# Three pieces of the expert behind a pair are worked between the pair's last two piece pairs

## The chip, the cores and the metric

The kernel runs on one core of one Trainium2 chip. Its time is device microseconds of one launch, and the numbers below are the median of three runs and one profiled execution.

## The reference

The program computes one block with four sequence mixers and a mixture of experts, and a second block behind it. The change touches the mixture alone. Of the reference that is:

```python
D_MODEL = 1024; SEQ = 512; N_EXPERTS = 32; TOP_K = 4; D_EXPERT = D_MODEL
SWIGLU_LIMIT = 7.0; SWIGLU_ALPHA = 1.702

def _moe_ffn(x2d, router_w, router_b, w_gu, b_gu, w_down, b_down):
    logits = (x2d @ router_w + router_b).astype(jnp.float32)
    top_val, top_idx = lax.top_k(logits, TOP_K)
    gate = jax.nn.softmax(top_val, axis=-1)
    ...
    def expert_block(args):
        xblk, e = args
        hg, hl = jnp.split(xblk @ w_gu[e] + b_gu[e], 2, axis=-1)
        hg = jnp.minimum(hg, SWIGLU_LIMIT)
        hl = jnp.clip(hl, -SWIGLU_LIMIT, SWIGLU_LIMIT)
        glu = hg * jax.nn.sigmoid(hg * SWIGLU_ALPHA)
        return ((hl + 1.0) * glu) @ w_down[e] + b_down[e]
    yb = lax.map(expert_block, (xb, block_expert)).reshape(n_rows, d)
    y = (yb * row_gate[:, None]).astype(x2d.dtype)
    return jnp.zeros((t + 1, d), x2d.dtype).at[row_tok].add(y)[:t]
```

Each token goes to 4 of 32 experts. An expert's weights are 1024x2048 and 1024x1024 floats, 12 MB, and all 32 experts' weights are read once: 384 MB.

## The kernel before

**Pieces.** An expert's weights come in 12 pieces of 1 MB (128 partitions x 2048 floats, CHUNKS = 12). Pieces 0 to 7 are the first product (banks `pu`, two pieces to a bank), pieces 8 to 11 the second (banks `pd`). Each expert gets a tile of 128 token rows; the few that need more have their other rows done elsewhere (`RestOfExperts`).

**Singles and pairs.** The 14 experts with the fewest tokens are worked two at a time: 64 rows for the left, 64 for the right, as fp32 products of half width straight from the loaded pieces. That is a *pair*, 24 pieces. The other 18 are *singles*. A single's piece is split first: ScalarE rounds it into `wh` (`high_part`), VectorE subtracts into `wl` (`low_part`), and TensorE adds up twelve products (`wh` and `wl` with `Xh`, `wh` with `Xl`). The order of units is ORDER = 4 x "sssp" + 3 x "ssp": 25 units, numbered by place from 0; the pairs stand at places 3, 7, 11, 15, 18, 21 and 24. A single that follows a pair is called `behind`; there are six. Places 4 to 15 are three turns of a loop.

**Buffers.** Eight slots hold loaded pieces (`raw` and a part of `y`, `slot_of`). A pair has eight more, `more_raw`, and these lie on the memory of `wh` and `wl`: slots 0 to 3 of `more_raw` are the four slots of `wh`, slots 4 to 7 those of `wl`. A pair's pieces 0 to 7 go to the eight slots, 8 to 15 to `more_raw`, 16 to 19 to four of the eight slots again, 20 to 23 to `more_raw` again (`pair_slot`). Piece pair 10 (pieces 20 and 21) lies on slot 2 of `wh` and `wl`, piece pair 11 (22 and 23) on slot 3.

**Queues.** SyncE issues all weight loads in one queue, in the order in which the code writes them, each behind a wait that says that its slot is free: `w_low` counts split pieces, `used` counts pieces (or piece pairs) that TensorE is done with, 12 in a unit. GpSimd issues, for each unit, one scatter of the last unit's rows to `y_rows`, one gather of the next unit's rows, and the next unit's bias rows. TensorE, ScalarE and VectorE each run their own list; `unit` in each block writes it. TensorE starts a unit with `biases`, then works piece by piece; `between` puts `slots` (the next unit's row numbers), two `turn_x` (transposes of the next unit's rows) and two `turn` (transposes of the hidden rows) between products. `turn(n, 0)` of a single stands in piece 5 and waits for `hb`, which VectorE writes in `valued` behind the split of piece 6.

## Time and profile before

| | us |
|---|---|
| runs (median of 3) | 3268.94 (3262.03 to 3270.54) |
| profiled execution, its own time | 3267.66 |
| its span | 3266.0 |
| mean granted TensorE clock | 0.984 of full speed |
| TensorE busy with products | 3103.1 (95%) |
| the mixture in it, from first weight load to last product | about 481 to 1538 |

The profile divides the span in 40 slices of 81.65 us; the mixture lies in slices 6 to 18. In the trace's answers times are microseconds from the start of the span. A timeline row gives start, duration, engine, line, operation, output and inputs, and in brackets how long the engine sat idle ahead of it and what ended that. "Issue" there means that the profile shows no releaser. Line 2464 is a weight load, 2649 to 2651 a single's products, 2668 and 2669 a pair's, 2756 the rounding on ScalarE, 2844 the subtraction on VectorE, 2610 a single's bias, 2588 `turn_x`, 2598 `turn`, 2764 the weighted rows of the last unit, 2852 and 2854 `valued`.

### The profile page before, as it was taken

What the parts mean: (1) busy time and instruction counts of PE and PEld (TensorE: products, weight loads), DVE (VectorE), ACT (ScalarE), POOL (GpSimd) and SP (SyncE); (2) the same over time, 40 slices, a digit from 0 to 9 for tenths busy, and PEclk for the clock granted to TensorE, in tenths of its full rate; (3) what the DMA queues carried; (4) which work ended last, traced back from release to release, by engine and by line L of the source; (5) the groups of instructions that cost most, each with busy time, mean ns of one, the idle gap of its engine ahead of it and who ended that gap; (6) DMA issues with size and microseconds to landing.
All of it is one profiled execution on the core that took longest, in us unless ns stands there. A gap on an engine that the chain in (4) does not pass through costs nothing. (4 is left out here: it accounts for less than half of the span.)

```text
span 3266.0 us, 47097 instructions
## 1 busy us (share of the span) xinstructions
PE 3103.1 (95%) x18657; PEld 2307.2 (71%) x18657; DVE 2036.6 (62%) x2537; ACT 1545.2 (47%) x1909; POOL 202.9 (6%) x199
## 2 busy tenths in 40 slices
PE   8998899999999999998999999999999999999998
PEld 6876567575757574664668777788877776778886
DVE  6744759484848483573568866666438876566533
ACT  4424437473737373462376355444226537344422
POOL 0000001121212121120000000000000000000000
PEclk9998999999999999999999999999999999999999
DMA  4112249999999999998122211232322221223331
GB/s 153 60 33 95 75 184 375 388 416 401 407 400 408 397 411 405 408 409 358 33 87 73 72 40 46 84 99 95 108 75 82 66 72 32 61 84 97 98 106 62
DMA packets 117303, 600.21 MB, mean 184 GB/s; under 512 B 19183, under 2 KB 22783, under 8 KB 66706
## 3 DMA queue, kind: packets, MB, share of 16 engines
q1 hardware_dynamic: 105442, 580.57, 46.6%
q0 software_dynamic: 11664, 16.89, 2.0%
q8 instruction: 138, 2.26, 0.3%
q14 instruction: 59, 0.48, 0.0%
HBM read 582.10 MB, written 26.28 MB: 186 GB/s over the span
## 5 line engine op out<-in xcount | busy, mean ns | idle before, releaser
L2844 DVE TENSOR_TENSOR wl<-raw,wh 128x2048 fp32r<-128x2048 f32 x166 | 378.3, 2287 | 65.4 <-ACT wh L2756 64.4
L2756 ACT ACTIVATE wh<-raw 128x2048 fp32r<-128x2048 f32 x166 | 318.1, 1917 | 123.5 <-DMA raw<-in_exp_w 66.4
L4784 ACT ACTIVATE w_high<-w_raw 128x1024 fp32r<-128x1024 f32 (+1 forms) x112 | 129.0, 1152 | 302.6 <-PE acc L4756 161.2
L4833 DVE TENSOR_TENSOR w_low<-w_raw,w_high 128x1024 fp32r<-128x1024 f32 (+1 forms) x112 | 150.0, 1339 | 180.0 <-PE ps L4714 94.7
L4736 PE MATMUL ps<-x_high,w_high 128*128 128x512 f32 x640 | 249.1, 389 | 0.0
L4737 PE MATMUL ps<-x_low,w_high 128*128 128x512 f32 x640 | 249.0, 389 | 0.0
L2649 PE MATMUL pu<-wh,Xh 128*128 128x512 f32 x576 | 233.4, 405 | 15.8 <-DVE wl L2844 15.8
L2651 PE MATMUL pu<-wh,Xl 128*128 128x512 f32 x576 | 227.9, 396 | 0.0
L2650 PE MATMUL pu<-wl,Xh 128*128 128x512 f32 x576 | 227.6, 395 | 0.0
L3581 PE MATMUL acc<-x_high,w_high 128*128 128x512 f32 x528 | 218.5, 414 | 1.5 <-ACT hq L3990 1.5
L3582 PE MATMUL acc<-x_low,w_high 128*128 128x512 f32 x528 | 206.5, 391 | 0.0
L4714 PE MATMUL ps<-x_high,w_low 128*128 128x512 f32 x704 | 173.1, 389 | 0.5 <-DVE w_low L4833 0.5
L4714 PEld LDWEIGHTS ps<-x_high,w_low 128*128 128x128 f32 x704 | 132.0, 188 | 28.7 <-DVE w_low L4833 1.3
L4258 DVE TENSOR_TENSOR w_low<-w_raw,w_high 128x1024 fp32r<-128x1024 f32 (+1 forms) x102 | 115.8, 1137 | 45.8 <-PE acc L3587 18.5
L2649 PEld LDWEIGHTS pu<-wh,Xh 128*128 128x128 f32 x576 | 110.1, 191 | 42.5 <-DVE wl L2844 17.7
L4749 PE MATMUL acc<-h_high,w_high 128*128 128x512 f32 x352 | 137.2, 390 | 1.8 <-DVE h_low L4867 1.8
L4736 PEld LDWEIGHTS ps<-x_high,w_high 128*128 128x128 f32 x640 | 120.1, 188 | 25.4 <-DVE cv L4844 0.4
L4737 PEld LDWEIGHTS ps<-x_low,w_high 128*128 128x128 f32 x640 | 120.1, 188 | 24.9
L4750 PE MATMUL acc<-h_low,w_high 128*128 128x512 f32 x352 | 137.0, 389 | 0.0
L3587 PE MATMUL acc<-x_high,w_low 128*128 128x512 f32 x528 | 133.7, 390 | 2.8 <-DVE w_low L4258 2.8
L2651 PEld LDWEIGHTS pu<-wh,Xl 128*128 128x128 f32 x576 | 110.0, 191 | 24.2
L3976 ACT ACTIVATE w_high<-w_raw 128x1024 fp32r<-128x1024 f32 (+1 forms) x101 | 99.1, 985 | 56.5 <-PE lev L3832 54.7
(934 smaller groups left out, 7212.9 us busy)
## 6 DMA issues: line engine op xcount, KB each, us to landing
raw<-in_exp_w SPq DMA_DIRECT2D x226, 1024.0 KB, 15.9
more_raw<-in_exp_w SPq DMA_DIRECT2D x84, 1024.0 KB, 17.6
y<-in_exp_w SPq DMA_DIRECT2D x74, 1024.0 KB, 16.2
w_raw<-in_w_in SPq DMA_DIRECT2D x100, 512.0 KB, 3.4
w_raw<-in_w_up SPq DMA_DIRECT2D x80, 512.0 KB, 3.7
w_raw<-in_w_down SPq DMA_DIRECT2D x32, 704.0 KB, 4.0
w_raw<-in_w_out SPq DMA_DIRECT2D x32, 384.0 KB, 3.1
kv_raw<-in_w_mem_kv SPq DMA_DIRECT2D x16, 512.0 KB, 3.7
```

Source lines behind the costliest of these rows:

```text
L2649: nc.tensor.matmul(o, lh[:, k, :], wh[:, m % PARTS, c], start=(m >= 8 and kh == 0 and kk == 0), stop=False)
L2650: nc.tensor.matmul(o, lh[:, k, :], wl[:, m % PARTS, c], start=False, stop=False)
L2651: mm = nc.tensor.matmul(o, ll[:, k, :], wh[:, m % PARTS, c], start=False, stop=end)
L2756: nc.scalar.activation(wh[:, m % PARTS, :], piece, ACT.Copy).then_inc(w_high, 1)
L2844: nc.vector.tensor_tensor(wl[:, m % PARTS, :], slot_of(n, m)[0], wh[:, m % PARTS, :], ALU.subtract).then_inc(w_low, 1)
L3581: nc.tensor.matmul(o, wh[:, n % 3, c], high[:, k, :], start=(k == 0), stop=False)
L3582: nc.tensor.matmul(o, wh[:, n % 3, c], low[:, k, :], start=False, stop=False)
L4714: mm = nc.tensor.matmul(o, wl[:, u % 2, c], high[:, k, :], start=False, stop=(k == DT - 1))
L4736: nc.tensor.matmul(o, wh(u)[:, c], high[:, k, :], start=(k == 0), stop=False)
L4737: nc.tensor.matmul(o, wh(u)[:, c], low[:, k, :], start=False, stop=False)
L4749: nc.tensor.matmul(o, wh(u)[:, c], hh[:, f * PART + k, :], start=(f == 0 and k == 0), stop=False)
L4833: nc.vector.tensor_tensor(wl[:, u % 2, 0:width(u)], raw_of(u), wh(u), ALU.subtract).then_inc(low_ready, 1)
```

## The change

For every pair but the last, pieces 0, 1 and 2 of the single behind it move into the pair's end, on all queues:

- SyncE loads piece 0 of the single ahead of the pair's pieces 20 and 21, and pieces 1 and 2 ahead of 22 and 23. It reads the single's expert number at the pair's start.
- TensorE works bias and piece 0 of the single ahead of piece pair 10, pieces 1 and 2 ahead of piece pair 11. `turn_x` for the single moves from behind piece pairs 8 and 9 to behind 7 and 8, `slots` for the next unit from behind piece 2 to ahead of piece 3.
- ScalarE takes `x_part` of the single ahead of `turned_part(n, 1)`.
- The counts that the splits wait for follow (`done`): the split of piece 2 still waits for piece pair 10, and the split of piece 3 for piece pair 11.

No piece, product or split is added or taken away.

```diff
--- before.py
+++ after.py
@@ -2303,6 +2303,9 @@
 FEW, WIDE = 2 * PAIRS, EXPERTS - 2 * PAIRS
 UNITS = WIDE + PAIRS
 HALF = SLOTS // 2
+EARLY = 3
+PAIR_END = CHUNKS - 2
+IN_FRONT = {PAIR_END: (0,), PAIR_END + 1: (1, 2)}
 SCATTERS = WIDE + 2 * (PAIRS - 1)
 ORDER = 4 * "sssp" + 3 * "ssp"
 ROUND_FROM, ROUNDS, ROUND_UNITS, ROUND_WIDE, ROUND_PAIRS = 4, 3, 4, 3, 1
@@ -2334,6 +2337,16 @@
     with eng.Fori(0, ROUNDS) as i:
         run(range(ROUND_FROM, ROUND_FROM + ROUND_UNITS), i)
     run(range(ROUND_FROM + ROUNDS * ROUND_UNITS, UNITS))
+
+
+def done(n, m):
+
+    first = n.at * CHUNKS
+    if n.pair and not n.last and m >= PAIR_END:
+        return first + (12, 15)[m - PAIR_END]
+    if n.behind and m < EARLY:
+        return first + (-1, 1, 2)[m]
+    return first + (m + 1)
 
 
 def mixture(K, a, x, place_y, gates, kept, saved, gain, shift):
@@ -2466,6 +2479,7 @@
                 def unit(n, following):
                     if n.pair:
                         left, right = expert_at(n.rank), expert_at(n.rank + 1)
+                        behind = None if n.last else expert_at(following.rank)
                         for c in range(2 * CHUNKS):
                             if c < RAW:
                                 sp.wait_ge(w_low, n.wide * CHUNKS + (c + CHUNKS - RAW + 1))
@@ -2474,11 +2488,15 @@
                             elif c < RAW + 2 * PARTS + 4:
                                 sp.wait_ge(used, n.at * CHUNKS + ((c - RAW - 2 * PARTS) // 2 + 1))
                             else:
+                                if not n.last and c % 2 == 0:
+                                    for m in IN_FRONT[c // 2]:
+                                        sp.wait_ge(used, n.at * CHUNKS + (m // 2 + 3))
+                                        chunk_in(behind, m, slot_of(following, m))
                                 sp.wait_ge(used, n.at * CHUNKS + (c // 2 - 3))
                             chunk_in(right if c % 2 else left, c // 2, pair_slot(n, c))
                         return
                     e = 0 if n.first else expert_at(n.rank)
-                    for m in range(CHUNKS):
+                    for m in range(EARLY if n.behind else 0, CHUNKS):
                         if m < RAW and n.behind:
                             sp.wait_ge(used, n.at * CHUNKS + ((m // 2 + 3 if m < 4 else m // 2 + 7) - CHUNKS))
                         elif m >= RAW or not n.first:
@@ -2631,11 +2649,11 @@
                         turn(n, 0)
                     if (m, kk) == (9, 0):
                         turn(n, 1)
-                    if not n.last and kk == 3:
-                        if m == 2:
+                    if following is not None and kk == 3:
+                        if m == 2 and not n.behind:
                             slots(following)
-                        if m in (8, 9):
-                            turn_x(following, m - 8)
+                        if m in ((7, 8) if n.pair else (8, 9)):
+                            turn_x(following, m - (7 if n.pair else 8))
 
                 def wide_chunk(n, following, m):
                     kh, g = halves(m)
@@ -2672,11 +2690,19 @@
                         between(n, following, m, kk)
 
                 def unit(n, following):
-                    biases(n)
-                    for m in range(CHUNKS):
+                    if not n.behind:
+                        biases(n)
+                    for m in range(EARLY if n.behind else 0, CHUNKS):
                         if n.pair:
+                            if m >= PAIR_END and not n.last:
+                                if m == PAIR_END:
+                                    biases(following)
+                                for early in IN_FRONT[m]:
+                                    wide_chunk(following, None, early)
                             pair_chunk(n, following, m)
                         else:
+                            if n.behind and m == EARLY:
+                                slots(following)
                             wide_chunk(n, following, m)
 
                 first = Unit(0)
@@ -2748,15 +2774,15 @@
                     piece, arrived, count = slot_of(n, m)
                     act.wait_ge(arrived, count)
                     if m >= PARTS:
-                        act.wait_ge(used, n.at * CHUNKS + (m - PARTS + 1))
+                        act.wait_ge(used, done(n, m - PARTS))
                     elif n.behind:
-                        act.wait_ge(used, n.at * CHUNKS + ((5, 6, 11, 12)[m] - CHUNKS))
+                        act.wait_ge(used, n.at * CHUNKS + ((5, 6, 12, 15)[m] - CHUNKS))
                     elif not n.first:
                         act.wait_ge(used, n.at * CHUNKS + (m - PARTS + 1))
                     nc.scalar.activation(wh[:, m % PARTS, :], piece, ACT.Copy).then_inc(w_high, 1)
 
-                def weighted(at, odd, d, split):
-                    act.wait_ge(used, at * CHUNKS + (11 + d))
+                def weighted(at, odd, d, split, behind=False):
+                    act.wait_ge(used, at * CHUNKS + ((12, 15) if behind else (11, 12))[d])
                     if d == 0:
                         act.wait_ge(returned, at + 1)
                         act.wait_ge(paid, at * 2 + 2)
@@ -2764,7 +2790,7 @@
                     nc.scalar.activation(to[:, odd, d * 512:(d + 1) * 512], pd[:, d, :], ACT.Copy, scale=gneg[:, odd:odd + 1]).then_inc(y_ready, 1)
 
                 def gate(n, c):
-                    act.wait_ge(used, n.at * CHUNKS + (4 * c + 2))
+                    act.wait_ge(used, done(n, 4 * c + 1))
                     nc.scalar.activation(rl[:, :], pu[:, 2 * c, :], ACT.Relu, scale=-1.0, bias=top[:, 0:1]).then_inc(relu, 1)
                     act.wait_ge(relu, n.at * 2 + (c + 1))
                     nc.scalar.activation(sg[:, :], rl[:, :], ACT.Sigmoid, scale=-SWIGLU_ALPHA, bias=top[:, 1:2]).then_inc(sigmoid, 1)
@@ -2795,16 +2821,16 @@
                                 x_part(n, 0)
                                 x_part(n, 1)
                             if m in ((0, 1) if n.pair else (2, 3)):
-                                weighted(n.at - 1, 1 - n.odd, m % 2, False)
+                                weighted(n.at - 1, 1 - n.odd, m % 2, False, n.behind)
                         if m in (5, 9):
                             gate(n, (m - 5) // 4)
                         if m == 8:
                             turned_part(n.at, 0, n.pair)
                     if n.pair:
-                        turned_part(n.at, 1, True)
                         if not n.last:
                             x_part(following, 0)
                             x_part(following, 1)
+                        turned_part(n.at, 1, True)
 
                 nc.scalar.activation(rl[:, :].rearrange("p (j g e) -> p j g e", j=NT, g=4),
                                      gates[:, :, :].unsqueeze(2).to_broadcast([P, NT, 4, EXPERTS]), ACT.Copy).then_inc(copied, 1)
```

TensorE at the end of the first pair (place 3) and the start of the single behind it, before (2668 and 2669 are the pair's products, 2649 to 2651 the single's):

```order
L2668 MATMUL pd<-more_raw,h_126 64x512
L2669 MATMUL pd<-more_raw,h_126 64x512
L2334 UNCONDITIONAL_BRANCH
L2334 ISA
L2603 ISA
L2610 MATMUL pu<-brow,ones_120 128x512 x4
L2642 ISA
L2649 MATMUL pu<-wh,Xh 128x512
L2650 MATMUL pu<-wl,Xh 128x512
L2651 MATMUL pu<-wh,Xl 128x512
```

and after, at piece pair 9 (its last products, the bias, the single's piece 0; 2686 and 2687 are the pair's products, 2667 to 2669 the single's):

```order
L2686 MATMUL pd<-y,h_126 64x512
L2687 MATMUL pd<-y,h_126 64x512
L2628 MATMUL pu<-brow,ones_120 128x512 x4
L2667 MATMUL pu<-wh,Xh 128x512
L2668 MATMUL pu<-wl,Xh 128x512
L2669 MATMUL pu<-wh,Xl 128x512
```

and further on, from the last products of piece 0 into piece pair 10:

```order
L2667 MATMUL pu<-wh,Xh 128x512
L2668 MATMUL pu<-wl,Xh 128x512
L2669 MATMUL pu<-wh,Xl 128x512
L2686 MATMUL pd<-more_raw,h_126 64x512
L2687 MATMUL pd<-more_raw,h_126 64x512
```

The bias and the single's first products stand ahead of the pair's last two piece pairs, and piece pairs 10 and 11 have the single's products around them.

ScalarE at the same place, before, from the pair's last `turned_part` (2776) over the single's rows (2786) to the splits of its pieces 0 to 2:

```order
L2776 ACTIVATE h_126<-pt 128x512
L2786 ACTIVATE Xh<-pu 128x512 x2
L2334 UNCONDITIONAL_BRANCH
L2334 ISA
L2753 ISA
L2756 ACTIVATE wh<-raw 128x2048
L2753 REGISTER_ALU
L2756 ACTIVATE wh<-raw 128x2048
L2753 REGISTER_ALU
L2756 ACTIVATE wh<-raw 128x2048
L2759 ISA
```

and after:

```order
L2812 ACTIVATE Xh<-pu 128x512 x2
L2802 ACTIVATE h_126<-pt 128x512
L2337 UNCONDITIONAL_BRANCH
L2337 ISA
L2779 ISA
L2782 ACTIVATE wh<-raw 128x2048
L2779 REGISTER_ALU
L2782 ACTIVATE wh<-raw 128x2048 x2
L2785 ISA
L2788 ISA
L2790 ACTIVATE y<-pd,gneg 128x512
```

The single's rows come ahead of the last `turned_part`, and three splits stand ahead of the first row of the pair's weighted output, where they also stood before.

SyncE at the end of the same pair, before (its pieces 19 to 21; 22 and 23 follow):

```order
L2464 DMA y<-in_exp_w 128x2048
L2464 ISA
L2464 DMA more_raw<-in_exp_w 128x2048
L2464 ISA
L2464 DMA more_raw<-in_exp_w 128x2048
```

and after:

```order
L2477 DMA y<-in_exp_w 128x2048
L2477 ISA
L2477 DMA raw<-in_exp_w 128x2048
L2477 ISA
L2477 DMA more_raw<-in_exp_w 128x2048
L2477 ISA
L2477 DMA more_raw<-in_exp_w 128x2048
L2477 ISA
L2477 DMA raw<-in_exp_w 128x2048
L2477 ISA
L2477 DMA raw<-in_exp_w 128x2048
```

The single's piece 0 is issued right behind the pair's piece 19, ahead of the wait for piece 20; its pieces 1 and 2 stand ahead of pieces 22 and 23, which come next.

## Rows read from the trace of the kernel before

**Rows 1.** The page: GB/s of each of 40 slices; the mixture is in slices 6 to 18.

```profile
GB/s 153 60 33 95 75 184 375 388 416 401 407 400 408 397 411 405 408 409 358 33 87 73 72 40 46 84 99 95 108 75 82 66 72 32 61 84 97 98 106 62
```

**Rows 2.** Busy time, granted clock, DMA share and GB/s by stretch.

```profile
core 0: us, PE busy (x) PEld busy (x) DVE busy (x) ACT busy (x) POOL busy (x), PEclk, DMA share, GB/s
...
608.00:1535.00 927.00, 881.97 (x4192) 560.32 (x4192) 553.24 (x494) 473.05 (x400) 166.36 (x157) 0.99 1.01 406
700.00:710.00 10.00, 10.00 (x49) 7.85 (x47) 8.93 (x6) 8.05 (x8) 2.78 (x1) 1.00 1.01 427
740.00:750.00 10.00, 10.00 (x57) 8.14 (x56) 8.72 (x7) 7.39 (x6) 4.09 (x2) 1.00 0.95 362
```

**Rows 3.** The page, DMA issues: count, KB each, median us from issue to landing.

```profile
raw<-in_exp_w SPq DMA_DIRECT2D x226, 1024.0 KB, 15.9
```

**Rows 4.** Loads issued in 730:767 and in 763:764, median to landing; all loads, min/median/max.

```profile
raw<-in_exp_w SPq DMA_DIRECT2D x10, 1024.0 KB, 11.6
...
raw<-in_exp_w SPq DMA_DIRECT2D x1, 1024.0 KB, 10.8
...
DMA to landing us min/median/max: 5.4/16.2/29.5
```

**Rows 5.** Timeline of TensorE, 805:827: piece pairs 8 to 11, then the single.

```profile
805.29 0.64 PE L2668 MATMUL pd<-raw,h 128*64 128x512 f32 x1 [1.28 <-issue]
...
810.15 0.61 PE L2668 MATMUL pd<-y,h 128*64 128x512 f32 x1 [0.62 <-issue]
...
815.06 0.64 PE L2668 MATMUL pd<-more_raw,h 128*64 128x512 f32 x1
...
819.94 0.61 PE L2668 MATMUL pd<-more_raw,h 128*64 128x512 f32 x1 [1.23 <-issue]
...
823.52 0.50 PE L2610 MATMUL pu<-brow,ones 32*128 32x512 f32 x4
826.71 0.79 PE L2649 MATMUL pu<-wh,Xh 128*128 128x512 f32 x1 [2.68 <-DVE wl L2844]
```

**Rows 6.** Busy time by unit: pair (place 7), then the singles at places 8, 9 and 10.

```profile
774.20:826.70 52.50, 46.26 (x224) 15.83 (x216) 8.34 (x13) 8.76 (x10) 4.82 (x6) 1.00 1.02 418
826.70:864.10 37.40, 37.38 (x168) 30.16 (x168) 36.93 (x29) 31.26 (x26) 9.22 (x7) 0.96 1.01 415
864.10:899.80 35.70, 35.70 (x172) 29.17 (x168) 34.28 (x28) 28.45 (x23) 7.64 (x6) 1.00 1.01 391
899.80:936.80 37.00, 37.00 (x196) 29.51 (x192) 28.71 (x26) 23.57 (x20) 9.65 (x10) 1.00 0.99 384
```

**Rows 7.** Timeline of SyncE: pieces 18 and 19, then 20 to 23 of the pair.

```profile
781.50 3.48 SPq L2464 DMA_DIRECT2D y<-in_exp_w  x2
800.09 4.94 SPq L2464 DMA_DIRECT2D more_raw<-in_exp_w  x4
```

**Rows 8.** Timeline of ScalarE: rounding of the single's piece 0.

```profile
822.42 1.91 ACT L2756 ACTIVATE wh<-raw 128x2048 fp32r<-128x2048 f32 x1 [6.65 <-DMA raw<-in_exp_w]
```

**Rows 9.** Timeline of VectorE: subtractions of pieces 0 and 1; `hb` of place 8.

```profile
824.36 4.71 DVE L2844 TENSOR_TENSOR wl<-raw,wh 128x2048 fp32r<-128x2048 f32 x2 [7.87 <-ACT wh L2756]
...
842.77 0.69 DVE L2854 SCALAR_TENSOR_TENSOR hb<-vc,sg 128x512 f32<-128x512 f32 x1
```

**Rows 10.** Timeline of TensorE: `turn` in piece 5, at place 4 and at place 8.

```profile
681.04 0.66 PE L2598 MATMUL pt<-const,hb 128*128 128x128 f32 x4 [1.05 <-DVE hb L2854]
...
843.26 0.39 PE L2650 MATMUL pu<-wl,Xh 128*128 128x512 f32 x1
843.49 0.39 PE L2651 MATMUL pu<-wh,Xl 128*128 128x512 f32 x1
843.72 0.60 PE L2598 MATMUL pt<-const,hb 128*128 128x128 f32 x4
...
845.55 0.40 PE L2649 MATMUL pu<-wh,Xh 128*128 128x512 f32 x1
```

**Rows 11.** Stretch 826:828, the first products of place 8.

```profile
826.00:828.00 2.00, 1.29 (x3) 1.10 (x4) 1.87 (x2) 1.46 (x2) 0.00 (x0) 0.57 1.00 422
```

## The prediction

> **What bounds the kernel now.** I read the GB/s by slice first [rows 1]. In the mixture, slices 6 to 18, it stands between 358 and 416 for thirteen slices in a row, where most of the rest has 30 to 110. So the question for any reordering of TensorE in this part is whether TensorE or the weight loads set its pace.
>
> Then the stretches [rows 2]. From 608 (the first pair) to 1535 (the last piece pair) the DMA share is 1.01 and the mean 406 GB/s. Where nothing but weights moves it is 427; where a scatter and a gather fall in, 362. So 427 looks like the full rate, and the mean is that rate less the row traffic. TensorE's own timeline gives the same rate: piece pairs 9, 10 and 11 of a pair start at 810.15, 815.06 and 819.94, after 805.29 for piece pair 8 [rows 5], 14.65 / 3 = 4.88 us for two pieces, 2.44 us a piece (1.049 MB / 2.44 us = 430 GB/s).
>
> Third, how deep the queue is. A weight load takes 15.9 us in the median from issue to landing [rows 3], and the shortest of all took 5.4 [rows 4]. The difference, 10.5 us, is some four pieces queued ahead. The queue is shortest late in the third single of a round: 11.6 us in the median at 730 to 767, one of 10.8 at 763 [rows 4]. Even there a load waits 10.8 - 5.4 = 5.4 us behind others. A queue that is never empty sets the time by its bytes.
>
> Last, the units [rows 6]. The singles take 37.4, 35.7 and 37.0 us with TensorE busy all along; the pair at place 7 takes 52.5 with TensorE busy 46.26, the one stretch in which TensorE waits. A round of three singles and a pair is 60 pieces: 60 x 2.44 = 146 us, and what is left of the round's 52.5 + 37.4 + 35.7 + 37.0 = 162.6 us is row traffic, some 16 / 4 = 4 us a unit. TensorE alone would need that less what it waits in the pair, 52.5 - 46.3 = 6.2 us, the wait ahead of the single among it. TensorE gets ahead of the loads by that much in a round and gives it up at the pair's end: 1.28 and 0.62 us ahead of piece pairs 8 and 9, 1.23 ahead of 11, 2.68 ahead of the single [rows 5].
>
> **The change, part by part.** Counts of products, splits and bytes stay as they are. What moves are places in three lists. I work through place 7 to place 8; the other five transitions have the same lists.
>
> *Loads.* Pieces 18 and 19 are issued at 781.5, piece 20 not until 800.09, behind its wait for TensorE [rows 7]. The single's piece 0 now goes out at about 785. That is free, and it gains nothing: the queue still holds pieces 16 to 19 at 800, so piece 0 only takes the landing slot of piece 20. The loads land in the order p19, s0, p20, p21, s1, s2, p22, p23, s3 (p of the pair, s of the single), one slot each 2.44 us. p19 lands by 810.1, when piece pair 9 starts, so s0 at 812.6, p21 817.5, s1 819.9, s2 822.4, p23 827.3, s3 829.7. The extra read of an expert number on SyncE stands where that queue has over 10 us in hand: nothing.
>
> *Splits.* Rounding takes 1.91 us [rows 8], the subtraction 4.71 / 2 = 2.35 behind it [rows 9]: 4.3 us from landing to product. Before, s0 was rounded at 822.42 and its products began at 826.71.
>
> *TensorE.* Products of a single start 0.23 us apart (843.26, 843.49 [rows 10]), so a piece is 12 x 0.23 = 2.75 us; a piece pair is 823.52 - 819.94 = 3.5 [rows 5]. Piece pair 9 with its `turn` (0.4) ends at about 814.1, the bias by 814.6. s0 can start at 812.6 + 4.3 = 816.9 and ends 819.6; piece pair 10 runs to 823.1; s1, landed 819.9, starts 824.2, ends 826.9. s2 landed at 822.4, but its place in `wh` is free only when piece pair 10 is done at 823.1, so it starts at 827.4 and ends 830.1. Piece pair 11 runs to 833.6. s3 landed at 829.7, but its place in `wh` lies under p22 and so under piece pair 11: 833.6 + 4.3 = 837.9. Before, s3 started three pieces behind 826.71, the first of them slow (below), at 826.71 + 3 x 2.75 + 1.7 = 836.7 (the unit took 37.4 us against 35.7 at place 9 [rows 6]). So filling the waits makes s3 1.2 us later: the waits were for loads, and the buffer that s3 needs is now given back last.
>
> *The splits behind it.* The head start that the splits had is gone too. `turn` in piece 5 needs `hb`, which stands on VectorE behind the splits of pieces 4, 5 and 6. From the end of s3's split at 837.9 these are 3 x 2.3 = 6.9. Five small ones stand between them and behind them; the last of these, `hb`, takes 0.69 [rows 9], and I take 2.4 for the five, an estimate: `hb` at 847.2. Before, `turn` ran on time at 843.72 and piece 6 started at 845.55, 1.83 later [rows 10]. Now piece 6 starts at 847.2 + 1.8 = 849.0, 3.5 us late. This wait has a precedent: at place 4, where the splits trailed the loads, `turn` waited 1.05 us for `hb` [rows 10].
>
> *Sum.* Each single behind a pair is 3.5 us late in its middle, six times. Does it reach the end? Late products free slots late, so loads are issued 3.5 us later in the next singles. The shortest lead there is 5.4 us over an unloaded transfer [rows 4], and 3.5 fits in it: the queue does not run dry, the loads land as before, and TensorE, late at the start of the next pair, meets the landing of piece pairs 7 and 8 with less wait. The term is 0 for each of the six, with the cover named: the queue's lead of 5.4 us. If it were gone all six would be paid, 6 x 3.5 = 21 us. `turn_x` one piece pair earlier lies in the same waits: 0. The end of the mixture is the last piece pair of place 24, which has no single behind it and lands when its bytes have come. Sum: 3267.7 + 0; with the median 1.3 us over the profiled execution, and half a microsecond for small losses, 3269.5.
>
> *A rule that speaks for the change.* At 826 to 828, behind the wait of 2.68 us, the granted clock was 0.57 [rows 11], between the two levels of 1.2 and 2.4 GHz, and the unit took 37.4 - 35.7 = 1.7 us longer than the next. The Trainium skill, "TensorE: Matmul & The Clock Gate", section "Why this matters for your kernels", advises against idle gaps between bursts of products since they bring the clock down. The trace agrees on the fall. By that rule alone the six gaps are worth closing, at most 1.7 us each, and the sum would be up to 6 x 1.7 = 10 us lower, 3259. By the rows above it is worth nothing, since 1.7 us less of TensorE are 1.7 us more of waiting for loads; and the change opens a gap as long ahead of s3 (833.6 to 837.9).
>
> **Rivals.**
>
> *Slower: the queue runs dry.* Mechanism: lateness of TensorE beyond the lead of the weight queue, in the third single of the rounds sssp. It decides from 5.4 us. My 3.5 are a sum of chained waits; if the clock also falls at s0 (its gap is 2.4 us, near the 2.68 that brought it down) everything behind it moves 1.7 us, to about 5; a place in the rounds with a shorter lead than the one row I have would do the rest. For it: the lead is one sample. Against it: the median of that stretch is 6.2 over unloaded. If each transition paid 1 to 3.5 us: 6 to 21 us, 3275 to 3290; middle 3281.
>
> *Faster: TensorE is what counts.* If the 406 GB/s were the demand of TensorE rather than the supply, filling 1.23 and 2.68 and the slow clock of 1.7, some 5 us for each of six, would give 30 us, 3239. Against it: the issue-to-landing times, and that TensorE waits at all for a load issued 15 us before (piece 20, 800.09 to 815.06 [rows 5, 7]). The milder form, the slow clock alone given back, is 3259 to 3262.
>
> *The order of loads costs or gains.* The interleaved loads might land in another rhythm beside gathers and scatters, which now fall some 3.5 us later. Bounds from the slowest and fastest rows: 362 against 427 over a few us a round, +-2 us in all. It stays inside the forecast.
>
> **How the numbers follow.** About 0.3% (9.8 us) is what a measurement of this kernel can tell from no change. Forecast, loads cover it: 3269.5, own range 3263 to 3275, chance 0.66. Queue runs dry: 0.24, of which a quarter stays within 0.3%. Faster: 0.10, of which the mild form, 0.04, stays within. So faster 0.06, same 0.66 + 0.06 + 0.04 = 0.76, slower 0.18. The range 3262 to 3284 leaves out the strong form of both.
>
> **What would show it.** In the profile after: TensorE's wait ahead of the single's first product falls under 2.5 us, and a new wait of about 4 us stands ahead of s3, released by VectorE's `wl`; `turn` in piece 5 waits 1 to 3 us for `hb`; the waits ahead of piece pairs 7 and 8 shrink by about 3.5 us; the single's middle is later against its pair by 3 to 4 us; the weight loads end within 2 us of 1535, as now. The mean of the mixture stays at 406 GB/s. Wrong would be: loads at the end of the third single with 5.4 us to landing, which is the queue run dry; or an end of the mixture over 5 us earlier, which would mean that the loads had been waiting for TensorE all along.

## The result and the profile after

The changed kernel takes 3273.8 us in the median of 20 runs (3268.52 to 3280.37), the kernel before 3267.2 in 20 runs beside it (3262.03 to 3271.86): ratio 1.0018, interval 1.0012 to 1.0024. It is slower by some 6 us (4 to 8). That lies inside 0.3%, and it is no zero. The forecast was 3269.5. The profiled execution took 3270.8 us, against 3267.7 before: a trace shows one execution, and the two compared below differ by 3.2 us.

From the page of the kernel after, the GB/s by slice and the loads into `raw` (count, KB, median us from issue to landing):

```profile
GB/s 153 60 33 97 76 184 377 393 398 390 405 394 404 392 408 413 401 414 382 33 87 72 68 43 44 86 97 97 108 73 84 66 72 31 60 84 97 97 106 61
...
raw<-in_exp_w SPq DMA_DIRECT2D x226, 1024.0 KB, 9.9
```

Against [rows 1] slices 8 to 13 are lower, 398 390 405 394 404 392 for 416 401 407 400 408 397, and slice 18, the last of the mixture, is higher (382 for 358): the same bytes, later. Against [rows 3] a load lands 9.9 us behind its issue instead of 15.9. Nothing became faster; fewer loads are queued ahead of each.

Stretches of the kernel after (columns as in [rows 2]):

```profile
608.00:1535.00 927.00, 881.88 (x4178) 556.47 (x4178) 551.33 (x492) 471.53 (x399) 165.65 (x157) 0.98 1.01 403
...
838.00:844.00 6.00, 2.46 (x6) 1.98 (x7) 4.73 (x3) 5.97 (x6) 2.23 (x1) 0.62 1.01 422
```

403 GB/s for 406, with TensorE's busy time unchanged (881.88, 881.97 before). Part of the loss stands where the queue was shortest. The third single of a long round (place 6), before and after:

```profile
737.23:774.24 37.01, 37.01 (x197) 29.50 (x193) 28.65 (x26) 23.50 (x20) 9.66 (x10) 1.00 0.98 383
```

```profile
742.30:779.31 37.01, 37.01 (x197) 29.50 (x193) 28.63 (x26) 23.50 (x20) 9.66 (x10) 1.00 0.99 370
```

The third singles at places 10 and 14 have 384 and 386 GB/s before, 379 and 374 after. The last singles of the short rounds (places 17, 20 and 23) lose as much, 395, 396 and 403 for 406, 411 and 413.

TensorE at place 7 and the single behind it: the first product of piece pair 9, the bias, pieces 0, piece pair 10, pieces 1 and 2, piece pair 11, piece 3, then `turn` in piece 5 and piece 6.

```profile
813.11 0.64 PE L2686 MATMUL pd<-y,h 128*64 128x512 f32 x1
...
817.43 0.51 PE L2628 MATMUL pu<-brow,ones 32*128 32x512 f32 x4
819.62 0.50 PE L2667 MATMUL pu<-wh,Xh 128*128 128x512 f32 x1 [1.68 <-DVE wl L2870]
...
822.55 0.64 PE L2686 MATMUL pd<-more_raw,h 128*64 128x512 f32 x1
...
826.13 0.50 PE L2667 MATMUL pu<-wh,Xh 128*128 128x512 f32 x1
...
830.61 0.50 PE L2667 MATMUL pu<-wh,Xh 128*128 128x512 f32 x1 [1.46 <-DVE wl L2870]
...
833.55 0.64 PE L2686 MATMUL pd<-more_raw,h 128*64 128x512 f32 x1
...
841.54 0.79 PE L2667 MATMUL pu<-wh,Xh 128*128 128x512 f32 x1 [3.80 <-DVE wl L2870]
...
850.68 0.66 PE L2616 MATMUL pt<-const,hb 128*128 128x128 f32 x4
...
852.57 0.40 PE L2667 MATMUL pu<-wh,Xh 128*128 128x512 f32 x1
```

Read it against [rows 5] from piece pair 9 on, which started at 810.15 before. Piece 3 stood at about 836.8 before, 26.6 behind it; now 841.54 - 813.11 = 28.4. Piece 6 stood at 845.55, 35.4 behind [rows 10]; now 39.5. So it is 4.1 us later, where 3.5 was forecast.

VectorE's `hb`, on which `turn` in piece 5 waits:

```profile
849.94 0.69 DVE L2880 SCALAR_TENSOR_TENSOR hb<-vc,sg 128x512 f32<-128x512 f32 x1
```

It ends at 850.6, and `turn` starts at 850.68.

Now TensorE's waits over 620 to 1535 (what waited, what for; us in total, times, longest), of the kernel before:

```profile
PE pd L2668 <- issue: 18.9, 20, 1.6
PE pu L2649 <- DVE wl L2844: 15.8, 6, 2.7
PE pu L2668 <- DMA more_raw<-in_exp_w: 9.1, 10, 2.5
```

and after:

```profile
PE pu L2667 <- DVE wl L2870: 41.7, 19, 3.9
...
PE pd L2686 <- issue: 1.9, 3, 1.3
```

The waits of a pair's products, 18.9 + 9.1 = 28 us, are down to 1.9. For the 18.9 the profile names no releaser; I take them for loads too, since they are gone where the loads are halved (e4, below). The waits for splits are up from 15.8 to 41.7. TensorE waits as long as before (these rows add up to 43.8 and 43.6, and `turn` waits another 1.0 and 1.3 for `hb`), but for its own order of work instead of for the loads. That is the sign of a bound that has changed hands.

The queue, at the same place as [rows 4] (loads issued in 735:772, the third single, now a little later):

```profile
raw<-in_exp_w SPq DMA_DIRECT2D x10, 1024.0 KB, 7.3
y<-in_exp_w SPq DMA_DIRECT2D x3, 1024.0 KB, 7.3
```

It was 11.6. Last, where it ends: first products of the pairs at places 7, 18 and 24, and of the last piece pair, before

```profile
774.24 0.64 PE L2668 MATMUL pu<-raw,X 128*64 128x512 f32 x1
...
1228.06 0.64 PE L2668 MATMUL pu<-raw,X 128*64 128x512 f32 x1
...
1487.18 0.64 PE L2668 MATMUL pu<-raw,X 128*64 128x512 f32 x1
...
1534.67 0.61 PE L2668 MATMUL pd<-more_raw,h 128*64 128x512 f32 x1 [1.28 <-issue]
```

and after

```profile
779.31 0.64 PE L2686 MATMUL pu<-raw,X 128*64 128x512 f32 x1
...
1237.24 0.64 PE L2686 MATMUL pu<-raw,X 128*64 128x512 f32 x1
...
1495.25 0.64 PE L2686 MATMUL pu<-raw,X 128*64 128x512 f32 x1
...
1538.54 0.61 PE L2686 MATMUL pd<-more_raw,h 128*64 128x512 f32 x1 [1.27 <-issue]
```

TensorE is 5.1 us late at place 7, 9.2 at place 18, 8.1 at place 24, and 3.9 at the last piece pair, ahead of which it waits 1.3 us in both. The account of where that comes from is below, behind the runs that it rests on.

### The profile page after: what moved, and what is told of

Same layout as the page of the kernel before. It is cut to its first block and busy times, and to the rows that moved or that the text cites. A ratio compares the mean times of both kernels' runs of the same rounds, so it can differ in the third digit from the quotient of the medians.

```text
span 3269.0 us, 47124 instructions
## 1 busy us (share of the span) xinstructions
PE 3105.2 (95%) x18657; PEld 2304.4 (70%) x18657; DVE 2035.5 (62%) x2537; ACT 1544.8 (47%) x1909; POOL 202.2 (6%) x199
## 5 line engine op out<-in xcount | busy, mean ns | idle before, releaser
L2667 PE MATMUL pu<-wh,Xh 128*128 128x512 f32 x576 | 237.0, 412 | 41.7 <-DVE wl L2870 41.7
L4810 ACT ACTIVATE w_high<-w_raw 128x1024 fp32r<-128x1024 f32 (+1 forms) x112 | 129.0, 1152 | 302.6 <-PE acc L4782 161.2
L2668 PEld LDWEIGHTS pu<-wl,Xh 128*128 128x128 f32 x576 | 111.4, 193 | 21.6
```

The costliest lines, as they stand in the source:

```text
L2667: nc.tensor.matmul(o, lh[:, k, :], wh[:, m % PARTS, c], start=(m >= 8 and kh == 0 and kk == 0), stop=False)
L2668: nc.tensor.matmul(o, lh[:, k, :], wl[:, m % PARTS, c], start=False, stop=False)
```

## The experiments

Each expectation names its own theories A and B. At the start, theory A is that TensorE comes late at each pair's end, through the chain of splits, by more than the queue's lead; theory B is that the new order of loads costs time by itself. The twelve runs come in four groups.

### How many pieces can be moved

The same change with two pieces (piece 0 ahead of piece pair 10, piece 1 ahead of 11) and with one. The diff is cut: the counts that the splits wait for follow, and `slots` stays ahead of piece 3.

```diff
-EARLY = 3
-IN_FRONT = {PAIR_END: (0,), PAIR_END + 1: (1, 2)}
+EARLY = 2                                            # e1
+IN_FRONT = {PAIR_END: (0,), PAIR_END + 1: (1,)}
+EARLY = 1                                            # e2
+IN_FRONT = {PAIR_END: (0,), PAIR_END + 1: ()}
```

> The change with two pieces of the single instead of three: piece 0 ahead of piece pair 10, piece 1 ahead of piece pair 11, piece 2 back behind the pair. Theory A (TensorE's lateness): the change costs time because piece 3's split waits for piece pair 11, which now stands behind pieces 1 and 2; the middle of the single is some 4 us late against the pair, and that is more than the lead of the load queue. With piece 2 behind piece pair 11, piece 3 starts about 3 us earlier against piece pair 9 (24.5 to 25.5 us behind its start, for 28.4 in the changed kernel and 26.6 in the kernel before), piece 6 at 36 to 37.5 (39.5 and 35.4). That fits in the lead: 3266 to 3269, no difference from before. Theory B (load order): interleaved loads cost DMA time by themselves; two of three pieces are still interleaved, so 2/3 of the 6 us stay: 3270 to 3272.

> The change with one piece instead of three (piece 0 ahead of piece pair 10, the others behind the pair). Theory A: piece 3 starts 24 to 25 us behind piece pair 9, piece 6 at 34 to 36 (35.4 before): 3265 to 3268, the same as before. Theory B: a third of the 6 us stays, 3269.

Two early: 3266.8, ratio 1.0004 (0.9995 to 1.0013). One early: 3267.6, 0.9999 (0.9990 to 1.0008). Neither is told from the kernel before. Behind the pairs at 7 to 21 piece 6 starts 36.8 to 38.5 us behind piece pair 9 with two, and 35.2 to 35.4 with one, as before (35.4 to 35.6); the last piece pair starts at 1533.89 and 1533.65. The third piece is what costs: it moves piece pair 11 from 17.8 to 20.4 us behind piece pair 9, and with it the return of piece 3's place in `wh`, so that piece 3 starts at 28.4 instead of 25.8. None of the three forms gains anything.

### Loads alone, and loads halved

The kernel before, with SyncE's new order alone:

```diff
+                                if not n.last and c % 2 == 0:
+                                    for m in IN_FRONT[c // 2]:
+                                        sp.wait_ge(used, n.at * CHUNKS + (m // 2 + 3))
+                                        chunk_in(behind, m, slot_of(following, m))
...
-                    for m in range(CHUNKS):
+                    for m in range(EARLY if n.behind else 0, CHUNKS):
```

> The kernel before with only SyncE's part of the change: pieces 0 to 2 of the single are loaded ahead of the pair's last pieces, all products and splits stay in their old order. Theory A: piece pairs 10 and 11 land one and three slots of 2.45 us later, pieces 0 to 2 are there by then; piece pair 11 ends at about +20.6 behind piece pair 9 for +13.2, the splits of pieces 0 and 1 are done early, piece 3 starts at 29 for 26.6, piece 6 at 38 for 35.4, 2.6 us late. That is inside the lead: 3266 to 3269. Theory B: the whole cost of the changed kernel, 3272 to 3275.

3271.8, ratio 1.0015 (1.0006 to 1.0024): theory A's number missed, B's reached at its edge. The trace tells how. Piece pairs 10 and 11 at place 7:

```profile
815.52 0.61 PE L2676 MATMUL pd<-more_raw,h 128*64 128x512 f32 x1 [0.72 <-issue]
...
825.28 1.08 PE L2676 MATMUL pd<-more_raw,h 128*64 128x512 f32 x1 [6.10 <-issue]
```

Pieces 22 and 23 now land three slots later, and nothing fills the time: TensorE waits 6.1 us, and the single's piece 6 comes 39.5 us behind piece pair 9, as late as in the changed kernel. The loads move 404 GB/s over the mixture, so no slower transfer is seen; I read their cost as TensorE's lateness, 4.1 us at piece 6 where theory A had 2.6. In the changed kernel pieces 0 to 2 fill this wait (it has none ahead of piece pair 11), so it is not to be added there. That the loads' order costs nothing at all beside the lateness is not shown.

Then both kernels with the loads into the eight slots of `raw` and `y` halved from place 4 on (`width[0]` is CW // 2 there; loads into `more_raw` stay whole). The other half of a slot keeps older weights, so the results are not the block's, and only the time is read. The diff is cut to the load:

```diff
-                    sp.dma_start(to, w[bass.ds(e, 1), m, :, :].rearrange("a p n -> (a p) n")).then_inc(arrived, 16)
+                    n = CW if any(arrived is s for s in more_loaded) else width[0]
+                    sp.dma_start(to[:, 0:n], w[bass.ds(e, 1), m, :, 0:n].rearrange("a p n -> (a p) n")).then_inc(arrived, 16)
```

> The kernel before with the loads into the eight slots halved from place 4 on (columns 0 to 1023 of a piece alone; the rest of a slot keeps old values, so the products take other numbers and the time is read without them). Loads of a round fall from 60 pieces to 36, 88 us for 154 of TensorE, so loads can't be the bound. It shows what TensorE alone would need with the old order. Theory A: all waits at the pair's end go, the mixture ends some 65 us earlier, 3200 (3190 to 3210).

> The changed kernel with the same halved loads. Theory A: the waits for splits inside the new order stay, since they are chains of ScalarE, VectorE and TensorE and no loads: piece 2's products wait 1.5 us for its split behind piece pair 10, piece 3 waits 4.4 us, piece 5's turn waits 1 to 3, with a fall of the clock; 9 us for each of six against the old order: 3250 (3238 to 3258), 45 to 60 us over the kernel before with halved loads. Theory B (load order costs, the order of products is harmless): equal to it within 6 us. A theory by which the change fills waits of TensorE: 10 us or more under it.

3207.2 (2 runs; ratio 0.9811, 0.9792 to 0.9831) and 3269.0 (1.0001, 0.9991 to 1.0012). One round, from the pair at place 11 to the pair at place 15, in the first and in the second:

```profile
924.06:1077.94 153.88, 153.88 (x753) 103.46 (x745) 108.11 (x94) 91.73 (x76) 31.53 (x29) 1.00 0.77 263
```

```profile
942.21:1106.74 164.53, 157.12 (x752) 104.12 (x745) 108.08 (x94) 91.72 (x76) 30.97 (x29) 0.99 0.72 245
```

This is the clearest result of the study. With the loads out of the way the old order needs 153.9 us for a round and TensorE never stops; the new order needs 164.5, 10.7 us more. Of these 6.9 are the three waits for splits (1.68, 1.46 and 3.80 us, ahead of pieces 0, 2 and 3), 1.6 is piece 3 at the lower clock (4.6 us for 3.0), 0.7 stands in piece 5, where `turn` waits 0.5 us for `hb`, and the rest is in small pieces. The changed kernel with all its loads needs the same 164.5 (943.84 to 1108.39). The kernel before, held by its loads, took 162.6 and 163.2. So the change spends all the room that TensorE had, and 1.3 to 1.9 us a round beyond it. Theory A had put the second kernel lower, 3238 to 3258, and missed: it underrated the size of the change's own cost, not its direction.

### Lateness by itself

Added products ahead of piece 1 of the single behind a pair make TensorE late, with loads, splits and order untouched: five of them, nine of them, nine in the three transitions of the long rounds (sssp), nine in the other three.

```diff
                         else:
+                            if n.behind and m == 1:                  # e8: and n.off < 96; e9: and n.off >= 96
+                                for _ in range(9):                   # e6: 5
+                                    K.keep_busy(pt[:, :], 512)
                             wide_chunk(n, following, m)
```

> The kernel before with five products of a constant (128x512, fp32, about 0.86 us each, 4.3 us in all) put on TensorE ahead of piece 1 of each single behind a pair: TensorE is late there by about as much as in the changed kernel, and the order of loads, splits and products is the old one. It adds 6 x 4.3 = 25.8 us of work to TensorE. Theory A: the queue's lead covers most of it, as in the changed kernel: 3269 to 3276, +2 to +8 us. If the lead covered nothing: 3293. Theory B: late products cost nothing since the load order is the old one, 3266 to 3268.

3267.1, ratio 0.9996 (0.9987 to 1.0005). Theory A's 3269 to 3276 missed. At place 16:

```profile
1151.99 0.50 PE L2649 MATMUL pu<-wh,Xh 128*128 128x512 f32 x1 [2.61 <-DVE wl L2847]
1154.86 4.46 PE L236 MATMUL pt<-const 128*128 128x512 f32 x10
```

Here the clock did not fall behind the wait of 2.61 us (piece 0 took 3.0 us, 4.6 before), so 1.6 us of slow clock were not paid. Behind the pairs at 18 and 21 the next single starts 56.5 us behind piece pair 9, for 54.0: 2.5 us late, not 4.3. The wait ahead of piece pair 6 takes most of that: it was 2.52 and 2.16 us in the pairs at 18 and 21, and is gone.

> The kernel before with nine such constant products (7.7 us) ahead of piece 1 of each single behind a pair, 46 us of TensorE work. Theory A: beyond a lead of some 3.7 us (10.8 us to landing at the shortest, less the 7.1 that a load takes when the queue is about empty) each us of lateness is paid in the rounds of three singles, and part of it in the others: 4 rounds x 4 = 16 us, 3283 (3277 to 3292). If the queue covered nothing: 3313. If it covered all: 3267.

3278.1, ratio 1.0027 (1.0017 to 1.0037), within the expectation. The next single starts 59.5 and 59.7 us behind piece pair 9 of the pairs at 18 and 21, for 54.0 and 53.9: 5.5 to 5.8 us late. And the last piece pair starts at 1542.98, 8.3 later than before.

> The kernel before with nine added fp32 products of 512 columns (7.7 us of TensorE) ahead of piece 1 of the single behind the pairs at places 3, 7, 11 and so in three of the six places that e7_late9 had them (4, 8 and 12). Theory A, each round by itself: a round's lateness is covered only by TensorE's waits in the same round. In the trace of before the pair's first piece to its piece pair 9 takes 33.06 us at place 3, which is what it takes with no wait, and 35.92, 36.39 and 36.89 at places 7, 11 and 15, against 38.80 and 38.45 at 18 and 21: so there are 0 to 3.8 us of waits in the long rounds (sssp) and over 5 in the short ones (ssp), and the products are some 5.5 us late. All of e7_late9's loss arises here: 3275 to 3279, ratio 1.0024 to 1.0036. Theory B, every late transition pays alike: half of the 8.9 us, 3271 to 3272.5. Theory C, the lateness is given back in the short rounds behind: 3266 to 3269.

> The same nine added products, but only at places 16, 19 and 22, behind the pairs at 15, 18 and 21. Theory A: the waits of these rounds (3.8, 5.7, 5.4 us ahead of piece pair 9, and 6.0 in the last pair) take the 5.5 us: 3266 to 3270, ratio within 1.0000 +- 0.001. Theory B, every late transition pays alike: 3271 to 3272.5. Theory C does not differ from A here.

3276.5, ratio 1.0025 (1.0017 to 1.0034), and 3268.6, 1.0005 (0.9996 to 1.0014). As theory A expected: all of the loss comes from the long rounds. Half each would be 1.0013, outside the first interval. Pairs at 15 and 18 and the last piece pair of the first:

```profile
1110.83 0.64 PE L2668 MATMUL pu<-raw,X 128*64 128x512 f32 x1
...
1233.44 0.64 PE L2668 MATMUL pu<-raw,X 128*64 128x512 f32 x1
...
1539.94 0.61 PE L2668 MATMUL pd<-more_raw,h 128*64 128x512 f32 x1 [1.27 <-issue]
```

TensorE is 10.7 us behind the kernel before at place 15 (1100.10 there). With the added products gone it makes up 5.3 us in one round, and then no more: +5.4 at place 18, +5.3 at the end. What it made up, I read as what the queue had held in hand; what stays, as time in which the queue was nearly empty. Loads issued in its third single at place 14 (1045.6:1078.3) land after 8.0 us in the median, 14.7 in the kernel before; at place 17 (1168.6:1201) it is 16.4 again, 16.0 before. In the second the last piece pair starts at 1536.79, 2.1 later.

### Clock and `hb`

The changed kernel with added products in the wait ahead of piece 3:

```diff
                             if n.behind and m == EARLY:
                                 slots(following)
+                                for _ in range(4):
+                                    K.keep_busy(pt[:, :], 512)
```

> The changed kernel with four added fp32 products of 512 columns (3.4 us) in the wait of 3.80 us ahead of piece 3 of the single behind a pair, so that TensorE does not stand idle there. In the trace of the changed kernel piece 3 takes 5.19 us where a piece takes 2.75, so 2.4 us per transition come from the clock. Theory A, a round's own length against the loads': the changed kernel's round of 164.5 us falls to 162.1, under the 162.6 to 163.2 that the loads need, so the loads set the pace again and only the first transition's lateness is left: mixture ends within 2 us of before, 3267 to 3270, ratio 1.0000 to 1.0009. Theory B, the slow clock is not on the chain (the splits of pieces 4 to 6 and hb set the end): round stays 164.5, 3273 to 3275, ratio 1.0018.

3273.6, ratio 1.0016 (1.0007 to 1.0025): theory B. Place 16 (the added products, piece 3, `turn` in piece 5):

```profile
1174.02 3.68 PE L236 MATMUL pt<-const 128*128 128x512 f32 x8
1178.02 0.50 PE L2667 MATMUL pu<-wh,Xh 128*128 128x512 f32 x1 [0.32 <-DVE wl L2872]
...
1187.11 0.66 PE L2616 MATMUL pt<-const,hb 128*128 128x128 f32 x4 [1.99 <-DVE hb L2882]
```

The clock stayed up and piece 3 took 3.0 us, for 4.5 at this place in the changed kernel, but `turn` then waited 1.99 us for `hb` (0.47 there), and piece 6 started 39.4 us behind piece pair 9, for 39.5. Places 4 and 22 read the same; at place 19 piece 0 ran at the lower clock (4.6 us), which puts everything behind it 1.6 us later, and from piece 3 on it reads the same too. Slow clock and `hb` lie side by side. (At places 8 and 12 of this execution TensorE stood 2.83 and 2.60 us ahead of `slots`, at the loop's jump, and the added products ran at half clock; it took 3281.5, 8 us over the median, and is read at the other places alone.)

Both at once, products behind the last piece pair and `turn` two pieces later, with halved and with full loads (the diff without the halving, which is as above):

```diff
-                    if (m, kk) == ((6, 1) if n.pair else (5, 1)):
+                    if (m, kk) == ((6, 1) if n.pair else (7, 1) if n.behind else (5, 1)):
...
+                    if n.pair and not n.last:
+                        for _ in range(4):
+                            K.keep_busy(pt[:, :], 512)
```

> The changed kernel with halved loads (as e5_half_after: from place 4 on, only half of each piece that goes to the eight slots of raw and y is loaded, the other half holds older weights), and with two edits: four products of 512 columns behind the last piece pair, in the wait ahead of piece 3, and turn 0 of the single behind a pair moved from piece 5 to piece 7. In e10_after_busy, at place 16, the products kept the clock at 1.00 and piece 3 took 3.02 us for 5.19, but then piece 5 took 5.55 us for 3.4, as turn 0 waited for hb, and piece 6 began at 39.4 us behind piece pair 9 as without them. Theory A, slow clock and hb stand side by side and each hides the other: with both taken away piece 6 begins some 2.5 us earlier, six times, 15 us: 3252 to 3258. Theory B, the splits of pieces 4 to 6 are as late as hb: 3266 to 3270, as e5_half_after.

> The changed kernel, all loads, with the same two edits. Theory A: the round of 164.5 us falls to 162.0, under the 162.6 to 163.2 that the loads need, so that only the first transition's lateness stays; 3267 to 3270, ratio 0.9999 to 1.0009. Theory B: as the changed kernel, 3272 to 3275, ratio 1.0018.

3292.4 (ratio 1.0072, 1.0057 to 1.0088) and 3295.2 (1.0081, 1.0067 to 1.0095): both theories missed, by over 20 us. The step that they were about went as A said: at the places where piece 0 ran at full clock, piece 6 starts 36.8 us behind piece pair 9, 2.7 earlier. What neither had looked at comes behind it. ScalarE, then TensorE, at place 12 of the second:

```profile
1024.96 0.60 ACT L2807 ACTIVATE hh<-pt 128x512 fp32r<-128x512 f32 x1 [4.99 <-PE pt L2616]
...
1028.61 5.49 ACT L2785 ACTIVATE wh<-raw 128x2048 fp32r<-128x2048 f32 x3
```

```profile
1034.21 1.11 PE L2616 MATMUL pt<-const,hb 128*128 128x128 f32 x4 [3.50 <-DVE hb L2883]
```

ScalarE's `turned_part` waits 4.99 us for the moved `turn`, with the splits of pieces 9 and 10 queued behind it; so the second `hb` is late, `turn` in piece 9 waits 3.50 us for it (as long at the other five places), and the next single starts 60 to 64 us behind piece pair 9 instead of 58. As a mend these two runs failed; they show only that slow clock and `hb` each hid the other.

## Why the forecast was near, and which step failed

**What bounds the kernel before: right.** Loads, from place 7 on. Halving them made it 61 us faster. The room was larger than I read: TensorE alone would need 153.9 us for a round, not the 162.6 - 6.2 = 156.4 that I took from its waits. Some 1.6 of the 2.5 between is the slow clock of piece 0 (4.4 to 4.6 us for 3.0), which goes with the wait.

**The timeline of a transition: right.** Behind piece pair 9, forecast and measured (the forecast's times less 810.15, the trace's less 813.11): piece 0 6.8 and 6.5, piece 2 17.3 and 17.5, end of piece pair 11 23.5 and 24.1, piece 3 27.8 and 28.4, `hb` written 37.1 and 37.5, piece 6 38.9 and 39.5. `turn_x`, put at 0, costs what it takes at the other end: with both halves ahead of piece pair 9, that one comes 33.80 us behind the pair's start instead of 33.06 where TensorE never waits. And piece 0 came as forecast for another reason than I gave: ScalarE's rounding had the single's rows and `turned_part` ahead of it, and a wait for `turn` between them, as these rows of the kernel after show:

```profile
813.22 0.60 ACT L2812 ACTIVATE Xh<-pu 128x512 fp32r<-128x512 f32 x1 [3.57 <-PE pu L2606]
814.81 0.60 ACT L2802 ACTIVATE h<-pt 128x512 f32<-128x512 f32 x1 [1.00 <-PE pt L2616]
815.33 1.91 ACT L2782 ACTIVATE wh<-raw 128x2048 fp32r<-128x2048 f32 x1
```

**`turn` waits 1 to 3 us for `hb`: wrong as a row, right as a bound.** Piece 3 ran at the slow clock (0.62 in 838:844) and took 5.2 us (4.5 to 5.5 at the six places), so `turn` came to `hb` just as it was ready; at three of the six places it waited 0.4 to 0.5 us. With the clock held (e10) the wait showed, 1.99.

**"The queue's lead of 5.4 us covers 3.5, the term is 0 for each of the six": this step failed.** The term was put at 0 and measured some 6 us (4 to 8). That 3273.8 still lies in the range of 3263 to 3275 is luck in part: the range reached 6 us to either side, as much as the whole effect. The size of the lead was good. The error is that it was set against each transition anew. The lead is one account for the whole chain: it is paid back only in rounds in which TensorE needs less than the loads do. Start of each pair against the kernel before, in us (from the first products, as shown for places 7, 18 and 24):

| pair at place | 3 | 7 | 11 | 15 | 18 | 21 | 24 | last piece pair | most late less end |
|---|---|---|---|---|---|---|---|---|---|
| after | -0.6 | +5.1 | +7.0 | +8.3 | +9.2 | +8.2 | +8.1 | +3.9 | 5.3 |
| e7, nine everywhere | -1.4 | +6.5 | +8.6 | +12.5 | +13.5 | +13.3 | +13.7 | +8.3 | 5.4 |
| e8, nine in long rounds | -1.9 | +5.1 | +9.1 | +10.7 | +5.4 | +5.1 | +5.1 | +5.3 | 5.5 |
| e9, nine in short rounds | -2.9 | -2.8 | -1.6 | -1.1 | +5.2 | +7.0 | +8.6 | +2.1 | 6.4 |
| e3, loads alone | -2.8 | +2.5 | +3.4 | +4.1 | +4.5 | +4.6 | +5.1 | +1.4 | 3.7 |
| e6, five everywhere | -3.3 | +1.4 | -0.3 | +2.9 | +0.9 | +1.0 | +1.4 | -1.1 | 4.0 |

Of the most that TensorE is ever late, 5.3 to 6.4 us do not reach the end in the four kernels that went beyond that, whatever made it late (5.3 in e10 and 6.7 in e12, which are not in the table). That I take for the lead. In the changed kernel the first transition fills the account, with 5.7 us from place 3 to place 7 (-0.6 to +5.1): in the kernel before TensorE did not wait in that pair (piece pair 9 stood 33.06 us behind its start), so there was nothing to take it. Up to place 11, 15 and 18 it then adds 1.9, 1.3 and 0.9. Behind that it adds nothing: the pairs at 18, 21 and 24 of the kernel before reached piece pair 9 5.4 to 6.0 us later than they do where TensorE never waits, and that room takes the lateness. Of the 9.2 us 3.9 are left at the end; with the 5.4 to 6.4 of the other three kernels it would be 2.8 to 3.8.

Each row is one execution, and the executions don't enter the mixture at the same time: the first product of place 0 stands 0.6 us (after) to 3.3 us (e6) ahead of that of the kernel before, and place 3 shows the same differences. Counted from its own start the mixture is 4.4 us longer in the changed kernel, 4.2 in e3, 2.2 in e6, and also 2.1 and 1.5 in e1 and e2, whose times are not told from the kernel before. So a figure of a row is good to some 2 us; the last column does not depend on the start. With that e3's 1.4 at the end and the 2 to 8 us of its timing are less at odds, but that only 3.7 of its lateness, and 4.0 of e6's, is taken is left open.

My own numbers would have come near this, as I see it afterwards. 3.5 us late, less the waits of 1.28 + 0.62 that I named as what shrinks, is 1.6 for each of the three transitions behind the first, and 3.5 for the first: 8.3, less the lead of 5.4, is 2.9 us, and the sum 3272.4.

**The lead's row.** 10.8 - 5.4 = 5.4 took the fastest of all loads as the unloaded one. With the queue nearly empty a load lands after 7.3 (above), not 5.4. By that row the lead at 763 was 3.5 us. The account of 5.3 is more than that. One reason may be that the queue was a little deeper in the later rounds: loads issued in 895:932 and 1058:1095 of the kernel before, the same place in the next two rounds, land after 12.4 and 12.1 us, 5.1 and 4.8 over 7.3. So the two slips of this term, the unloaded load and the one sample, went against each other.

**The clock gate.** The fall did not go away, it moved from piece 0 (0.57 in [rows 11]) to piece 3 (0.62). And there were five falls, not six: in the kernel before piece 0 took 3.0 us at place 4, behind a wait of 2.72. The Trainium skill, "TensorE: Matmul & The Clock Gate", section "Why this matters for your kernels", advises against idle gaps between bursts of products; going by that alone I had put closing all six at no more than 10 us. Here held clock bought nothing where it was tried: in e10 `hb` took its place. That in the kernel before the loads would have taken it was not tried.

**The rivals.** "The queue runs dry" is what happened, in a form milder than its 3275 to 3290: the loads of the third single land at 7.3 us. The sign named for it was 5.4, which was not reached; by the row of a nearly empty queue it should have read 7. It named "lateness beyond the lead" and decided from 5.4; it was the sum over rounds that passed 5.4. "TensorE is what counts" fell with the halved loads: the kernel before gets 61 us faster by them, so the loads had set its pace, and where nothing but TensorE and the splits count the new order is 62 us longer than the old one, not shorter. "The order of loads costs" was held to 2 us; alone it costs 2 to 8, through 6.1 us of wait at piece pair 11 that the changed kernel fills.

**What would show it.** The wait ahead of the single's first product under 2.5 us: yes, 1.7. The single's middle 3 to 4 us later: yes, 4.1. Waits ahead of piece pairs 7 and 8 gone: yes. A wait of about 4 us ahead of piece 3 by `wl`: yes, 3.80. Weight loads ending within 2 us of 1535 and 406 GB/s: no, 3.9 us later and 403.

## What to carry to other kernels

Where a transfer queue sets the pace, compare for each repeating round what the engine needs by itself with what the queue needs; the engine may grow up to that and not one microsecond beyond, since the excess comes back every round. A queue's lead covers a sum of latenesses once, not each of them. A first round in which the engine does not wait for the queue has no room to take any (place 3 to 7 here, 5.7 us). Halving the transfers in both kernels reads the two needs directly, and here it turned a difference of 6 us in 3270 into one of 62.

## What was not expected of the hardware

The same wait did and did not bring the clock down. In the changed kernel TensorE waits 1.65 to 1.82 us ahead of piece 0 at each of the six places, and the piece takes 3.0 us. In the last run (e12) it waits 1.65 to 1.69, and the piece takes 3.0 at places 4, 12 and 19, but 4.6 at 8, 16 and 22. In the kernel before, 2.72 at place 4 left the piece at 3.0 us and 2.58 at place 16 brought 4.6; in e6 a wait of 2.61 at place 16 left the clock at full speed, where 2.68 had brought 0.57 in [rows 11]. So 1.6 us each time hang on something that these traces don't show, and a sum should carry them as a bound.
